# Five low parts moved to GpSimd at the start of the first expert pass, and a new row schedule: one core, product-key experts in split fp32

## The reference, cut to what matters

```python
q = einsum(xt, peer_wq)                       # queries of 8 heads, 2 halves
s = einsum(q, peer_subkeys)                   # 128 + 128 scores a head
sv, si = top_k(s, 16); cand = sv0 + sv1       # 256 pairs
cv, ci = top_k(cand, 16); expert = i1 * 128 + i2     # 16 of 16,384 experts a head
gate = softmax(cv)
a = gelu(einsum('td,thkd->thk', xt, expert_u[expert]))
out = einsum('thk,thkd->td', gate * a, expert_v[expert])
```

## Time and profile before

| | |
|---|---|
| median of 3 runs | 1700.57 us (1699.0 to 1701.43) |
| the profiled execution, its own time | 1702.96 us |
| its span | 1701.3 us |
| PE busy | 97% |
| DVE busy | 80% |
| POOL busy | 29% |
| first expert pass (first L2018 to first L2047) | 519.33 to 1157.04 us of the span |

### The profile page before, as it was taken

One profiled execution on the slowest core, in us unless ns is written; L12 is line 12 of the kernel. 1 busy time (PEld: TensorE's weight loads), 2 busy tenths in 40 slices (PEclk: granted clock), 3 DMA queues, 4 the chain that ended last, 5 costly groups with the idle time before them and its releaser, 6 DMA issues.

```text
span 1701.3 us, 29339 instructions
## 1 busy us (share of the span) xinstructions
PE 1658.4 (97%) x10256; PEld 1564.8 (92%) x10256; DVE 1369.2 (80%) x2823; ACT 732.1 (43%) x1387; POOL 489.4 (29%) x454
## 2 busy tenths in 40 slices
PE   8998999988999999999999999999999999999999
PEld 6877766678999999999999999999998999999999
DVE  3273456766788999999999988877998999999996
ACT  2121354443224433666656667843333333333332
POOL 0003222211000233223322243342443444444440
PEclk9998999999999999999999999999999999999999
DMA  7517223313224898898988899998999999999994
GB/s 221 191 43 245 76 70 118 94 36 121 75 76 130 283 335 289 288 321 291 332 317 319 314 330 333 343 377 324 346 390 358 364 401 393 400 395 399 398 394 151
DMA packets 187429, 454.16 MB, mean 267 GB/s; under 512 B 25666, under 2 KB 91714, under 8 KB 186818
## 3 DMA queue, kind: packets, MB, share of 16 engines
q1 hardware_dynamic: 110850, 242.39, 40.4%
q0 software_dynamic: 50416, 182.63, 29.2%
q10 hardware_dynamic: 26016, 27.27, 4.7%
HBM read 401.14 MB, written 54.47 MB: 268 GB/s over the span
## 4 chain that ended last, share of the span: by engine, by line
PE 60%; DVE 5%; DMA 3%; issue 1%; ACT 0%; SPq 0%; POOL 0%; DVEq 0%; POOLq 0%; ACTq 0%
PE ps L2047 9%; PE ps L2053 9%; PE ps L2050 9%; PE ps L2023 9%; PE ps L2019 9%; PE ps L2018 9%; PE ps L2069 5%; DVE sb_w_lo L1848 1%; DMA sb_ring<-expert_v 1%; DVE sb_slot L1885 1%; DMA sb_expert_row<-expert_u_rows,sb_row_expert 1%; DMA sb_scores<-expert_u_rows,sb_row_expert 0%; DMA sb_expert_row<-expert_v,sb_row_expert 0%; DVE sb_scores L1969 0%; DVE sb_rows_y L1980 0%
## 5 line engine op out<-in xcount | busy, mean ns | idle before, releaser
L1753 ACT ACTIVATE sb_w_hi<-sb_ring 128x1024 fp32r<-128x1024 f32 x254 | 269.5, 1061 | 507.7 <-PE ps L2053 226.3
L1848 DVE TENSOR_TENSOR sb_w_lo<-sb_ring,sb_w_hi 128x1024 fp32r<-128x1024 f32 x255 | 311.8, 1223 | 57.1 <-ACT sb_w_hi L1753 55.7
L2018 PE MATMUL ps<-sb_x_hi,sb_w_hi 128*128 128x384 f32 x1024 | 350.3, 342 | 1.0 <-PEq L1255 1.0
L2019 PE MATMUL ps<-sb_x_lo,sb_w_hi 128*128 128x384 f32 x1024 | 345.9, 338 | 0.0
L2023 PE MATMUL ps<-sb_x_hi,sb_w_lo 128*128 128x384 f32 x1024 | 202.1, 339 | 5.1 <-DVE sb_w_lo L1848 5.1
L2047 PE MATMUL ps<-sb_x_lo,sb_w_hi 128*128 128x384 f32 x1016 | 197.8, 336 | 6.5 <-ACT sb_x_lo L1762 6.5
L2050 PE MATMUL ps<-sb_x_lo,sb_w_lo 128*128 128x384 f32 x1016 | 197.1, 336 | 0.0
L2053 PE MATMUL ps<-sb_x_lo,sb_w_hi 128*128 128x384 f32 x1016 | 197.1, 336 | 0.0
L2018 PEld LDWEIGHTS ps<-sb_x_hi,sb_w_hi 128*128 128x128 f32 x1024 | 192.0, 188 | 1.3 <-issue 1.3
L2019 PEld LDWEIGHTS ps<-sb_x_lo,sb_w_hi 128*128 128x128 f32 x1024 | 192.3, 188 | 0.0
L2023 PEld LDWEIGHTS ps<-sb_x_hi,sb_w_lo 128*128 128x128 f32 x1024 | 182.0, 188 | 6.4 <-DVE sb_w_lo L1848 6.4
(11 more groups left out here) (337 smaller groups left out, 2499.9 us busy)
## 6 DMA issues: line engine op xcount, KB each, us to landing
sb_ring<-expert_u SPq DMA_DIRECT2D x128, 512.0 KB, 6.2
sb_ring<-expert_v SPq DMA_DIRECT2D x128, 512.0 KB, 8.2
gates_dense<-sb_g_stage ACTq DMA_DIRECT2D x12, 2048.0 KB, 18.3
hid_dense<-sb_hid SPq DMA_DIRECT2D x104, 192.0 KB, 5.0
sb_scores<-hid_dense SPq DMA_DIRECT2D x104, 192.0 KB, 7.3
sb_g_stage<-gates_dense SPq DMA_DIRECT2D x32, 384.0 KB, 6.5
sb_g_stage<-gates_dense SPq DMA_DIRECT2D x48, 256.0 KB, 8.4
sb_ring<-peer_wq SPq DMA_DIRECT2D x16, 512.0 KB, 3.6
```

Of the source, the lines that this page charges most:

```text
L1753: nc.scalar.activation(whi[v % 2][:, :], ring(v)[:, :], ACT.Copy).then_inc(w_hi, 1)
L1848: nc.vector.tensor_tensor(wlo[v % 2][:, :], ring(v)[:, :], whi[v % 2][:, :], ALU.subtract).then_inc(w_lo, 1)
L2018: nc.tensor.matmul(out, hi[:, c * P:(c + 1) * P], g.x_hi[:, c], start=(c == 0), stop=False)
L2019: nc.tensor.matmul(out, hi[:, c * P:(c + 1) * P], g.x_lo[:, c], start=False, stop=False)
```

## The change

The five low parts of units 2 to 6 are made by POOL, ahead of its first gather, with a semaphore of their own (`lo_by_pool`). PE and SP wait for that semaphore in those units, and DVE leaves them out. To have a semaphore free, the two of the quarter rows (`quad_in`, `quad_moved`) become one, which counts to 64. `ROW_PLAN` gets other points: 1.19 rows a unit up to unit 104 (before: 1.20 up to 98, then 2.0), then 25 rows in 12 units, and 22 in the 11 units 117 to 127 (before: 17).

```diff
-ROW_PLAN = ((9, 0), (98, 107), (116, 143), (127, NR), (131, NR), (247, 2 * NR))
+ROW_PLAN = ((9, 0), (104, 113), (116, 138), (127, NR), (131, NR), (247, 2 * NR))
+POOL_LO = range(2, 7)
...
+        lo_count = lambda v: v + 1 - AHEAD_LO - (len(POOL_LO) if v > POOL_LO[-1] else 0)
+        lo_of = lambda v: (lo_by_pool, v - POOL_LO[0] + 1) if v in POOL_LO else (w_lo, lo_count(v))
...
                 if v >= NRAW + AHEAD_LO:
-                    sp.wait_ge(w_lo, v - NRAW + 1 - AHEAD_LO)
+                    sp.wait_ge(*lo_of(v - NRAW))
...
-                        sp.dma_start(moved[q - 1], quad_y[NQR * q:NQR * (q + 1), :]).then_inc(quad_moved, 16)
+                        sp.dma_start(moved[q - 1], quad_y[NQR * q:NQR * (q + 1), :]).then_inc(quad_in, 16)
...
         def _(pool):
+            for v in POOL_LO:
+                pool.wait_ge(w_hi, v + 1 - AHEAD_U)
+                pool.wait_ge(mm, v - 1)
+                pool.tensor_tensor(wlo[v % 2][:, :], ring(v)[:, :], whi[v % 2][:, :], ALU.subtract).then_inc(lo_by_pool, 1)
             pool.wait_ge(row_ready, 1)
...
-                dve.wait_ge(quad_moved, 48)
+                dve.wait_ge(quad_in, 64)
...
             for v in range(NV):
-                if v + 1 < NV:
+                if v + 1 < NV and v + 1 not in POOL_LO:
                     prepare_weights(v + 1)
...
                 if u >= AHEAD_LO:
-                    pe.wait_ge(w_lo, u + 1 - AHEAD_LO)
+                    pe.wait_ge(*lo_of(u))
```

More of the change, by code:

```diff
@@ L1663, in experts @@
         masks, hots, g_mm, g_out = map(sem, ("masks", "hots", "g_mm", "g_out"))
-        row_ready, row_used, dots_act, quad_in, quad_moved, quad_added = map(sem, ("row_ready", "row_used", "dots_act", "quad_in", "quad_moved", "quad_added"))
+        row_ready, row_used, dots_act, quad_in, quad_added, lo_by_pool = map(sem, ("row_ready", "row_used", "dots_act", "quad_in", "quad_added", "w_lo_by_pool"))
         y_mm, y_add = map(sem, ("y_mm", "y_add"))
@@ L2037, in v_unit @@
                 if u == NU - 1:
-                    pe.wait_ge(w_lo, v + 1 - AHEAD_LO)
+                    pe.wait_ge(*lo_of(v))
                     pe.wait_ge(c_l, u + 1)
```

## The result

| | kernel before | changed kernel |
|---|---|---|
| median, first comparison (5 and 5 runs) | 1699.38 us | 1707.15 us |
| median, repeated later (35 and 12 runs) | 1698.57 us | 1707.4 us |
| ratio, first and repeated | | 1.0049 [1.0031, 1.0067], 1.0044 [1.0025, 1.0063] |
| span of the profiled executions | 1701.3, 1704.7 us | 1703.0, 1704.2 us |

What follows compares the result with a forecast made beforehand. PE, busy 97% of the span, was taken as the bound, so only its waits, clock and matmul spacing could give time. -1.26 - 4.04 + 9.0 = +3.7 us gave a median of 1704.3 us, range 1695.5 to 1710.

Steps and rivals of the forecast that it cites:

- The end of the pass: Units 120 to 129: two rows a unit make low parts late, costing 9.0 us, bounds 2 and 13.
- The working by the round of a tile: From unit 120: four rows take 10.2 us, so 5.1 us a unit against 4.24; 7.9 us lost.
- The working by bytes: From unit 120: gathers, store and gate reads share 394 GB/s of queue traffic; 8.4 us lost.
- Unit 5: First pass: POOL's low parts remove PE's wait behind DVE's look-up, gaining 1.26 us, bounds 0 and 1.26.
- Units 31 and 33: Waits at look-ups: unit 31 less late, unit 33 as late as before; 0 gained.
- Unit 104: PE's wait for a late gathered row and the half clock behind it vanish: 4.04 us gained, bounds 2.3 and 4.04.
- Matmul spacing: Either pass: spacing might change by 1.3 to 6 us either way; taken as 0, with a wider range.
- (2): Units 120 to 129: waits long enough to halve the clock, or POOL issues late; 13 us, 1708.3 us total, chance 0.15.
- (3): Units 2 to 6: POOL and DVE block each other, adding 1.3 to 3 us, 1706; chance 0.42 together with main case.
- (1): Late units of the pass: gathers keep up, late part 0 to 2 us, 1696.3 us total, chance 0.20.
- (4): Both ends even out: late part 4 to 7 us, 1699.3 to 1702.3 us total, chance 0.23.
- L: Follow-up theory on the pass's end: a gather takes 8 us however few are in flight, so the 10.2 us round sets the rate.

Runs made afterwards that it cites:

- after: The changed kernel, in its first profile, compared with the kernel before: 1707.15 us, ratio 1.0049.
- experiment 5: Changed kernel with three gathers in flight instead of four for the 22 rows of iterations 117 to 127: 1721.54 us, ratio 1.0104.
- experiment 6: Changed kernel with the last store of the gates cut from 2 MB to 256 KB, the rest filled twelve units earlier with wrong data: 1705.76 us, ratio 1.0017.
- experiment 1: Kernel before with the new row plan alone, DVE still making all low parts: 1710.67 us, ratio 1.0067.
- after again: The changed kernel run once more, unchanged, for a second profile: 1707.4 us.
- experiment 4: Changed kernel with SP issuing the first four pieces of the gates behind the weights of unit 127, not ahead: 1709.99 us, ratio 1.0051.
- experiment 2: Changed kernel with the old row plan, so POOL's five low parts alone: 1698.63 us, ratio 0.9995.
- experiment 3: Changed kernel with the old row plan from unit 116 on and six rows more done by unit 104: 1697.18 us, ratio 0.998.
- experiment 7: Changed kernel with one row a unit up to unit 33, 1.34 up to 104, two up to 116, then the old rest: 1698.43 us, ratio 0.9993.
- experiment 8: Changed kernel with the last 22 rows of the first table spread over units 117 to 131 instead of 117 to 127: 1712.06 us, ratio 1.0056.
- before again: The kernel before run against itself, unchanged, for a second profile: 1700.9 us, ratio 1.001.
- experiment 10: As experiment 9, with the row plan evened out (25 rows to unit 33, 1.30 a unit to 104, 1.9 to 116, 1.33 to 131): 1700.66 us, ratio 0.9998.
- experiment 9: Experiment 8 with the SP order of experiment 4, the quarter sums' load four units later, second table's rows from unit 135: 1703.95 us, ratio 1.0021.

## Why the prediction was right, and where its terms were off

The forecast was 1704.3 us in a range of 1695.5 to 1710; 1707.15 and 1707.4 were measured. The cause and the direction were right. The size was not: +3.7 us were forecast, and +7.5 to +8.3 came. The time lies inside the range because the range is 14.5 us wide.

One sign of being right did not come. Unit 128 was to start 3 to 5 us later in the span, and it starts 0.9 us earlier (1156.12 against 1157.04), because unit 0 starts 3.35 us earlier in that trace. Counted from unit 0 to unit 128, the two traces of after take 640.1 and 638.8 us and those of before 637.7 and 633.8: 3.7 us more on average.

- **The end of the pass, +9.0.** Right in cause and, within 1.3 us, in size. The two traces of after take 59.6 and 60.3 us, the two of before 51.7 and 52.8: +7.7 us. The working by the round of a tile gave 10.2 us for four rows and a loss of 7.9 us; the four rounds measured 8.8 to 11.0 and 10.0 on average. The working by bytes gave 8.4, but experiments 5 and 6 speak against it: 1.8 MB less left 2.5 us a row, and one gather less in flight made it 3.13. What PE would wait for was only half right. In which units the late rows are paid differs from run to run (low parts in experiment 1, weights at 127, the product of unit 128), and the sum doesn't, because DVE's last row sets it. So the half clock inside this stretch is no extra: with 6.83 us of it (after), 3.41 (after again) or none (experiment 1) it is 59.6 to 60.3 us.
- **Half clock behind unit 128, taken as 0 in the sum.** The wait at unit 128 is 1.2 to 3.4 us with the new end against 1.2 to 2.5 with the old one, and in three of its four traces here the clock is halved behind it, where nothing takes the time back. The second trace of after, where PE had just waited 2.70 us:

```profile
1156.74:1160.15 3.41, 3.41 (x13) 3.41 (x12) 3.21 (x6) 0.62 (x2) 1.76 (x2) 0.50 1.04 411
```

  From unit 128 to 131 it takes 12.65 us without a fall (after) and 14.14 (after again), 14.13 (experiment 1) and 15.27 (experiment 4) with one; the five traces with the old end (before twice, experiments 2, 3 and 7) take 12.65 to 12.80. That is 0 to 2.6 us, +1.3 on average.
- **Unit 5, -1.26.** Right: -1.2 to -1.7 by units 0 to 9, part of it the shorter spacing (4.19 us a unit). POOL's price of 2.8 us was 2.4. The Trainium skill, "GPSIMD Engine Reference", section "Elementwise — side-by-side cycle accounting", is nearer with the 2.2 estimated from its 2.6 cycles an element. The blocking, forecast at 2 to 5 us, was 6.4; that DVE was in time for unit 7 all the same (by 1.3 us) was closer than forecast.
- **Units 31 and 33, 0.** Mis-sized. The sum of rows is the same, but one moved from iteration 29 to 31, and so from ahead of the wait at unit 31 to between it and unit 33. The prediction took unit 33 to be as late as before. PE's wait there:

```profile
659.78 1.68 PE L2030 MATMUL ps<-sb_x_hi,sb_w_lo 128*128 128x384 f32 x8 [1.96 <-DVE sb_w_lo L1855]
```

  It is 1.80 to 1.96 us in all eight traces with the new plan up to unit 104, and 0.75 to 0.82 in the six others; the two waits together grow by only 0.2 us. But in five of the eight (experiments 1, 4, 5, 6 and 8) the clock then fell, as in experiment 1:

```profile
664.72:668.13 3.41, 3.41 (x12) 3.41 (x12) 3.34 (x7) 0.91 (x1) 2.67 (x2) 0.50 0.91 267
```

  and in none of the six. From unit 9 to 36 these five take 117.2 to 118.4 us and the other three 115.9 to 116.2. That is 1.7 us, five times in eight: about +1.3 us with the 0.2. The changed kernel's own two traces are among the three without it.
- **Unit 104, -4.04.** The step that failed most: it took a stall of one execution for one of the kernel. The three traces with the old plan lose 4.03, 0 and 1.97 us there, 2 on average. The gain is so much smaller, and experiment 3, which has the gains at 5 and 104 without the new end, is 3.4 us under before by its ratio and not 5.3, though its interval holds both.
- **The sum.** -1.3 + 1.3 - 2.0 + 7.7 + 1.3 = +7.0 us in place of +3.7. Measured is +7.5 by the ratio, between 4.2 and 10.7. The terms are averages of two to eight traces, some from other kernels with the same plan, so that they meet the measured value this closely is in part luck.
- **Matmul spacing, taken as 0.** It is no effect of the change, but the largest difference between executions. From 1400 to 1500 us, deep in the second pass, before and before again, after:

```profile
1400.00:1500.00 100.00, 100.00 (x579) 100.00 (x578) 92.56 (x110) 36.79 (x49) 46.68 (x34) 1.00 1.02 395
```

```profile
1400.00:1500.00 100.00, 100.00 (x568) 100.00 (x567) 90.70 (x108) 36.55 (x48) 43.23 (x33) 1.00 1.02 392
```

```profile
1400.00:1500.00 100.00, 100.00 (x574) 100.00 (x574) 91.98 (x109) 36.44 (x48) 43.09 (x33) 1.00 1.03 395
```

  PE is never idle in any of them, at full clock, and starts 579, 568 or 574 matmuls. The second pass of one kernel takes 536.8 or 546.3 us.

Of the rivals, (2) had the half clock right. At unit 127 it costs nothing of its own; behind unit 128 it does, and at unit 33, where no rival looked for it, it follows waits of under 2 us. (3), a stall by POOL and DVE, didn't occur; (1) and (4) are out by the 7.7 us.

**What stays open.** Why the last store of 2 MB takes anything from 19 to 30 us where SP waits for it. With an eighth of the bytes (experiment 6) its packets were done within 8 us. In the changed kernel from 1135 to 1140 us, all queues together:

```profile
DMA packets 391, 1.25 MB, mean 250 GB/s; under 512 B 49, under 2 KB 69, under 8 KB 390
...
q0 software_dynamic: 268, 0.94, 53.4%
...
q10 hardware_dynamic: 24, 0.02, 1.2%
```

The store's last 24 packets, 20 KB, are still under way there, while the queues move 250 GB/s. That a few of the 16 engines are behind with gathers and hold the last packets is my reading; no run tested it. The Trainium skill, "DMA: Bandwidth & Descriptors", section "Queues, rings and completion order", says that each engine takes packets from its queues in turn, which would let the store's share depend on packet sizes; no run here varies them. More row tiles, the direct test of L, wasn't tried: there is no room for a fifth.

## What to carry to other kernels

Before a stall is booked as a gain, look for it in a second profile of the same kernel: the 4 us at unit 104 were there once in three traces. Where buffers in flight set a rate (here four tiles, 10 us a round, two of them asked for every 4.2 us), the delay is fixed by the last transfer, and taking away one of PE's waits for it only moves the wait. And an engine that is lent work can cost another more by blocking it (6.4 us) than it saves it (5.7 us); what helped was the order, not the load.

## What the runs showed of the hardware

- Matmuls of 384 columns follow each other in one of three spacings (173.3, 174.7 and 176.7 ns by the starts of the weight loads), which can hold for hundreds of us; between the slowest and the fastest lie 1.9% of a stretch that PE bounds. Most changes are at waits, not all: in experiment 4 the weight loads in 100 us fall from 573 to 567 between 1560 and 1580 us, with no PE wait after 1372.
- GpSimd's subtraction of 128x1024 blocks VectorE's bf16 instructions of only 128x128 too: 0.29 us became 2.38.
- After PE waits of 1.80 to 1.96 us at unit 33 the clock was halved for 3.41 us in five traces of eight; it stayed at 1.00 after waits of 2.30 and 2.47 us at unit 128 (before again, experiment 2) and fell after one of 2.70 (after again).
- The same 2 MB store was landed 19.3 to 29.7 us after its issue, by the end of SP's wait for it (experiments 10 and 9). With 256 KB in its place no packet of it was left after 8 us (experiment 6).
